# Two attention loops: one group of filler products per round, second-half value products issued in the next round

## What is computed

```
# first block, per block of 128 queries, branches c, s, w
p = softmax(where(mask, q @ k.T * scale, NEG));  o_b = p @ v
o = g[0] * o_c + g[1] * o_s + g[2] * o_w
mix = sigmoid(gate_a) * (o @ w_proj_a) + sigmoid(gate_b) * (ret_out @ w_proj_b)
# second block
p = softmax(q @ k.T * scale + F[q] - F[k]);  ya = p @ v           # fox, causal
sel = top_k(sum_h iw * relu(iq @ ik.T), 128);  yb = softmax(q @ k[sel].T * scale) @ v[sel]   # dsa
merged = sigmoid(ga) * (ya @ w_br_fox) + sigmoid(gb) * (yb @ w_br_dsa)
```

## Time and profile before

| | us |
|---|---|
| median of 3 runs (lowest, highest) | 2024.86 (2023.76, 2025.74) |
| the profiled execution | 2024.89 |
| its span in the trace | 2022.7 |
| TensorE busy | 1979.8 |
| VectorE, ScalarE, GpSimd busy | 930.9, 729.3, 794.3 |
| first attention, on TensorE | about 222.8 to 382.1 |
| second attention, on TensorE | about 1370.3 to 1534.7 |

### The profile page before, as it was taken

One profiled execution on the slowest core, in us unless ns is written; L12 is line 12 of the kernel. 1 busy time (PEld: TensorE's weight loads), 2 busy tenths in 40 slices (PEclk: granted clock), 3 DMA queues, 4 the chain that ended last, 5 costly groups with the idle time before them and its releaser, 6 DMA issues.

```text
span 2022.7 us, 25626 instructions
## 1 busy us (share of the span) xinstructions
PE 1979.8 (98%) x9324; PEld 1564.7 (77%) x9324; DVE 930.9 (46%) x1506; ACT 729.3 (36%) x1203; POOL 794.3 (39%) x329
## 2 busy tenths in 40 slices
PE   7999999999999999999999999999999999999998
PEld 6777666688888888888888887775757888888887
DVE  6763566432642563567761105586992341101111
ACT  5233455433431332332323224526453342221321
POOL 4365321243554345344543443231113434444442
PEclk9999999999999999999999999999999999999999
DMA  6345111243666477548533342231112424343341
GB/s 180 84 124 137 42 42 43 48 105 103 170 157 193 125 182 200 138 128 211 164 96 89 92 111 70 56 84 42 37 48 53 106 71 103 84 115 90 87 111 55
DMA packets 154565, 211.14 MB, mean 104 GB/s; under 512 B 15432, under 2 KB 129640, under 8 KB 154344
## 3 DMA queue, kind: packets, MB, share of 16 engines
q1 hardware_dynamic: 140232, 167.34, 33.1%
q10 hardware_dynamic: 14240, 42.54, 7.0%
HBM read 206.69 MB, written 2.10 MB: 103 GB/s over the span
## 4 chain that ended last, share of the span: by engine, by line
PE 49%; issue 31%; POOL 12%; DVE 7%; ACT 1%; DMA 0%; POOLq 0%; ACTq 0%; DVEq 0%
PE ps L628 15%; PE ps L630 15%; PE ps L629 15%; POOL wlo L594 12%; DVE top L2266 1%; DVE score L2268 1%; DVE ps L2157 1%; PE ps L1085 1%; PE ps L1108 0%; PE ps L719 0%; DVE PT L1987 0%; DVE Pb L1987 0%; PE ps L1311 0%; PE ps L1128 0%; DVE st L1902 0%
## 5 line engine op out<-in xcount | busy, mean ns | idle before, releaser
L594 POOL TENSOR_TENSOR wlo<-raw,whi 128x1024 fp32r<-128x1024 f32 (+1 forms) x317 | 784.0, 2490 | 1175.2 <-ACT whi L1377 1152.8
L628 PE MATMUL ps<-hhi,whi 128*128 128x512 f32 x1488 | 589.4, 396 | 6.6 <-DVE hlo L1896 2.7
L630 PE MATMUL ps<-hhi,wlo 128*128 128x512 f32 x1488 | 580.7, 390 | 0.0
L629 PE MATMUL ps<-hlo,whi 128*128 128x512 f32 x1488 | 580.2, 390 | 0.0
L1377 ACT ACTIVATE whi<-raw 128x1024 fp32r<-128x1024 f32 x309 | 316.9, 1055 | 378.9 <-PE ps L630 368.2
L628 PEld LDWEIGHTS ps<-hhi,whi 128*128 128x128 f32 x1488 | 280.0, 188 | 71.9 <-issue 9.9
L630 PEld LDWEIGHTS ps<-hhi,wlo 128*128 128x128 f32 x1488 | 279.7, 188 | 59.3
L629 PEld LDWEIGHTS ps<-hlo,whi 128*128 128x128 f32 x1488 | 280.1, 188 | 57.3 <-issue 1.4
L628 PE MATMUL ps<-hidhi,whi 128*128 (+1 forms) x608 | 236.6, 389 | 0.0
L630 PE MATMUL ps<-hidhi,wlo 128*128 (+1 forms) x608 | 236.5, 389 | 0.0
L629 PE MATMUL ps<-hidlo,whi 128*128 (+1 forms) x608 | 236.5, 389 | 0.0
(11 more groups left out here) (376 smaller groups left out, 2374.1 us busy)
## 6 DMA issues: line engine op xcount, KB each, us to landing
raw<-in_ffn_w SPq DMA_DIRECT2D x264, 256.0 KB, 3.8
raw<-in_w_in SPq DMA_DIRECT2D x154, 256.0 KB, 3.9
trig<-in_ada_w ACTq DMA_DIRECT2D x72, 512.0 KB, 4.7
raw<-in_w_up SPq DMA_DIRECT2D x64, 256.0 KB, 3.9
raw<-in_w_down SPq DMA_DIRECT2D x64, 256.0 KB, 4.0
raw<-in_w_out SPq DMA_DIRECT2D x32, 256.0 KB, 3.7
xrow<-in_x ACTq DMA_DIRECT2D x4, 512.0 KB, 6.8
raw<-in_cmp_k_w SPq DMA_DIRECT2D x8, 256.0 KB, 3.7
```

Source lines behind the costliest of these rows:

```text
L594: last = pool.tensor_tensor(lo, src, hi.bitcast(F32), ALU.subtract)
L628: pe.matmul(out_, lhi, rhi, start=first, stop=False)
L629: pe.matmul(out_, lhi, rlo, start=False, stop=False)
L630: return pe.matmul(out_, llo, rhi, start=False, stop=last)
```

## The change

Only TensorE's two loops over rounds are changed. In each round all four quarters (all of a round's quarters in the second attention, from round 2 on) go between the transposes and the values of the first half. The values of the second half of a round are put in a list, `late`, and issued in the next round, after its scores of pair 0 and ahead of its first transposes; what is left after the last round is issued at the end. In the second attention the order of index units is as before. No other engine's program is touched.

```diff
--- before.py
+++ after.py
@@ nsa_attention
                 n = len(UNITS1)
+                late = []
                 for r in range(n + 2):
                     nb = BLOCKS1[r - 2] if r >= 2 else 0
+                    half = (nb + 1) // 2
                     if r < n:
                         score_pair(r, 0)
                         if r == 0:
                             head_sum(3)
-                    half = (nb + 1) // 2
-                    for part, blocks in enumerate((range(half), range(half, nb))):
-                        if part == 1 and r < n:
-                            score_pair(r, 1)
-                            if r == 0:
-                                root_spread(3)
-                        for j in blocks:
-                            turn(r - 2, j)
-                        if r < n:
-                            branch_b(r, 2 * part, 2 * part + 2)
-                        for j in blocks:
-                            values(r - 2, j)
+                    for u, j in late:
+                        values(u, j)
+                    for j in range(half):
+                        turn(r - 2, j)
+                    if r < n:
+                        branch_b(r, 0, 4)
+                    for j in range(half):
+                        values(r - 2, j)
+                    if r < n:
+                        score_pair(r, 1)
+                        if r == 0:
+                            root_spread(3)
+                    for j in range(half, nb):
+                        turn(r - 2, j)
+                    late = [(r - 2, j) for j in range(half, nb)]
+                for u, j in late:
+                    values(u, j)
@@ fd_attention
                 n = len(UNITS2)
+                late = []
                 for r in range(n + 2):
                     nb = BLOCKS2[r - 2] if r >= 2 else 0
                     quarters = 4 * (FILL2[r + 1] - FILL2[r])
+                    half = (nb + 1) // 2
+                    first = quarters // 2 if r < 2 else quarters
                     if 2 * r < len(UNITS):
                         index_unit(2 * r)
                     if r < n:
                         score_pair(r, 0)
-                    half = (nb + 1) // 2
-                    for part, blocks in enumerate((range(half), range(half, nb))):
-                        if part == 1:
-                            if 2 * r + 1 < len(UNITS):
-                                index_unit(2 * r + 1)
-                            if r < n:
-                                score_pair(r, 1)
-                        for j in blocks:
-                            turn(r - 2, j)
-                        filler(r, quarters * part // 2, quarters * (part + 1) // 2)
-                        for j in blocks:
-                            values(r - 2, j)
+                    for u, j in late:
+                        values(u, j)
+                    for j in range(half):
+                        turn(r - 2, j)
+                    filler(r, 0, first)
+                    for j in range(half):
+                        values(r - 2, j)
+                    if 2 * r + 1 < len(UNITS):
+                        index_unit(2 * r + 1)
+                    if r < n:
+                        score_pair(r, 1)
+                    for j in range(half, nb):
+                        turn(r - 2, j)
+                    filler(r, first, quarters)
+                    late = [(r - 2, j) for j in range(half, nb)]
+                for u, j in late:
+                    values(u, j)
```

## The result

The changed kernel takes 2063.9 us (median of 4 runs, 2063.24 to 2066.05) against 2025.3 us before (2023.76 to 2026.12): 1.0197 times, 95% interval 1.0184 to 1.0209. It is 38.6 us slower. The profiled execution has a span of 2063.9 us and ran in 2066.05 us.

What follows compares the result with a forecast made beforehand. It took TensorE alone to bound the first attention, and VectorE and TensorE in turns the second. The first's 27.7 - 4.8 - 2.8 = +20.1 us and the second's +8.2 were added to 2024.9, giving 2053 us, range 2045 to 2062.

Steps and rivals of the forecast that it cites:

- wide range of 2037 to 2068: Whole kernel: the range in us said to take the forecast, rival 1 and the lower half of rival 2.
- rival 2: Both attentions: TensorE's clock falls in the stalls, 4 to 12 times at 1.7 us, 2060 to 2073, say 2065; chance 0.14.
- waiting scores: Each round's first score pair waits for the third exponential of the round before; 0.8 to 1.7 us each in the first attention.
- The stalls of the first attention: Rounds 1 to 22: TensorE's waits before first scores, 14.0 us without second-half transposes and 13.8 with them, 27.7 in sum.
- Both paths: What releases the awaited exponential: ScalarE's copies with second-half transposes (1.65 us stall, widest round), VectorE's reduction without (1.72).
- The merges: Two groups of quarter products become one, 2.93 us for 3.14; 4.8 us gained in 24 rounds of the first attention.
- Rounds 24 and 25: End of the first attention: no first scores and the same order of products as before, so no stall was counted.
- stall of 2.00 us without a fall: One TensorE stall in the earlier trace, up to 1484.60 us, with no clock fall after it; cited against rival 2.
- The second attention: VectorE's reductions come late from round 5, by 6.7 us in round 13; rounds 15 to 17 add about 1.5; +8.2 us.
- Rival 1: Second attention: VectorE hides the stalls and only round 5's 2 us stay; 2047 us; chance 0.17.
- Rival 3: First scores do not wait, so only the merges and the idle won back count, -7.6 us; 2017 us; chance 0.04.
- Rival 4: Whole kernel: the reorder does not reach the bound, stalls being about as large as gains; 2025 us; chance 0.02.

Runs made afterwards that it cites:

- first_only: The changed kernel with the earlier loop put back in the second attention, so only the first has the new order; 2051.85 us, ratio 1.0132.
- exp_first: The changed kernel with ScalarE's two exponentials ahead of its copies of the transposes in the second half, both attentions; 2055.3 us, ratio 1.0155.
- values_ahead: The changed kernel with the late second-half values issued ahead of the next first scores, in both attentions; 2049.74 us, ratio 1.0128.
- second_only: The changed kernel with the earlier loop put back in the first attention, so only the second has the new order; 2036.57 us, ratio 1.0059.
- dummies: The changed kernel with three useless products ahead of each first score pair of the first attention from round 1; 2059.11 us, ratio 1.017.
- dummies_both: The changed kernel with three useless products ahead of the first scores in both attentions; 2058.81 us, ratio 1.0171.
- three_one: The changed kernel with new order in the first attention only, its quarters split three and one around the second-half transposes; 2032.9 us, ratio 1.0049.

## Why the prediction was right, point by point

The forecast was 2053 us, in a range of its own of 2045 to 2062; measured were 2063.9, 1.9 us above that range. Only the wide range of 2037 to 2068, which takes in half of rival 2, holds it, and the number is nearer to rival 2's 2065. The direction and the mechanism of the waiting scores held. The size was 10 us too low, since four terms all erred to one side: the clock in the first attention (5.6 us, in no sum of the forecast), the end of that stage (1.4, put at nothing), the clock in the second, and the late waits there (together 4.2 by the profile).

- **The stalls of the first attention.** 27.7 us worked out, 27.8 measured, each kind within 0.03 us. The straight line between 31 and 512 keys held: 0.99, 1.23, 1.48 expected, 1.00, 1.24, 1.48 found. Both paths, copies and reduction, are shown apart by turning ScalarE's order round.
- **The merges.** A group of twelve takes 2.93 us (227.00 to 229.93), as worked out. The 24 groups take 74.1 us, 3.8 of them for the falls of the clock that run through three groups, and the 48 of before 75.7. So 5.3 us were gained where 4.8 were worked out.
- **"Rounds 24 and 25 ... their order of products is the same as before."** This step failed, by 1.4 us: the order of the two rounds is the same, but what stands ahead of them is not. Round 23's second group had stood between its exponentials and round 24. Now T1 follows S1 directly, and its copies stand behind two exponentials and the split of a slab on ScalarE. V1 waits 2.73 us, 1.29 before. ScalarE, then TensorE:

```profile
399.85 0.68 ACT L1568 ACTIVATE trig<-ps,nmax 128x512 f32<-128x512 f32 x1
...
400.51 1.05 ACT L1392 ACTIVATE whi<-raw 128x1024 fp32r<-128x1024 f32 x1
401.46 1.08 ACT L1576 ACTIVATE Pb<-ps 128x512 f32<-128x512 f32 x2
...
402.11 1.52 PE L1005 MATMUL ps<-Pb,vrow 128*64 128x256 f32 x8 [2.73 <-ACT Pb L1576]
```

- **The clock of the first attention** was left out of the forecast and priced as rival 2. It fell four times, for 5.6 us together, where the text said 4 to 12 times at 1.7 us over both attentions. The price was somewhat high: a fall takes 1.2 to 1.6 us, since part of the low stretch lies in a stall. The mistake was in the weight. The stall of 2.00 us without a fall was one case, and 22 waits give a fall many occasions; and of the three falls in the second attention of before the prediction read one (1421.8) and passed over the other two (1370.7 and 1503.8). Its sign for rival 2, a mean clock below 0.95, did not show either: four falls in this stage are a mean of 0.96. With the falls the stage closes: 27.8 - 4.8 - 2.8 + 1.4 + 5.6 = 27.2, and 27.1 were measured (26.7 with the 5.3 us measured for the merges).
- **The Trainium skill's rule** ("TensorE: Matmul & The Clock Gate", "A second HAM failure mode: psum-queue depth-cycling") spoke against the change, and this case's traces bear it out in part: the clock fell behind recurring idle of 0.8 to 1.7 us before the scores, and not there when useless products filled most of it. It is not regular: such falls are three in the change, two in first_only, one in exp_first and none in values_ahead, which idles for 23.4 us in the stage, the change for 28.0.
- **The second attention.** 8.2 us expected, 12.4 found (12.7 in second_only; 12.1 by its median). VectorE's first lag, in round 5, was given as 2.8 us and is 2.9; rounds 6 to 11 as 2.2, 2.9, 4.2, 5.5, 6.0, 6.0, and they are 2.3, 3.2, 4.7, 5.9 (second reduction of 8), 6.6, 6.8, all counted from round 4. The rest comes in rounds 12 to 15. In round 12 TensorE had waited 2.79 us for VectorE's selection, the clock fell, and the 24 products in one group ran through it; VectorE then waited 3.82 us, where 0.7 had been allowed for. TensorE, then VectorE:

```profile
1519.66 1.65 PE L1092 MATMUL ps<-dkT,dqT 64*128 64x384 f32 x4 [2.79 <-ACT trig L1631]
...
1529.98 0.92 PE L1092 MATMUL ps<-dkT,dqT 64*128 64x384 f32 x4
...
1531.03 0.57 DVE L2172 CUSTOM_DVE_ANT_0 ps<-ps,sel 128x384 f32<-128x384 f32 x1 [3.82 <-PE ps L1092]
```

  The lag is 10.6 us behind this, 11.7 in the second half of round 14, 13.7 in that of round 15 and 14.4 at the end of the stage, where 6.7 and some 1.5 more had been worked out. Less the 2.0 us by which rounds 0 to 3 are shorter than in before's trace (1.5 of them its own fall of the clock), these are the 12.4. S0 to S1 is 10.3 us in round 12 instead of the 7.4 of my terms. Before, that wait was 2.00 us and brought no fall, and only half the group stood between the two. A wait of VectorE of 2.6 us in this round is in second_only, dummies, dummies_both, values_ahead and exp_first too, each with S0 to S1 at 9.1 us and one fall of 3.4 us in that round, where the change has one of 6.8. So it is no accident of one run. That the clock makes the wait is read from the traces, not shown by an experiment: no kernel with the merged groups runs this round at the higher clock throughout.
- **Rival 1**, that VectorE hides the second attention, is out: second_only is 12 us above before, and 2 were its price. **Rival 3** is out: no stall was shorter than its chain. **Rival 4** as well. **Rival 2** is in part what happened, as said above.

## What to carry to other kernels

A group of filler between two steps of a chain is there for its place, not for its sum: before merging two groups, take from the trace the time from one step to the next (here 1.15 to 3.56 us) and look at what stands between them afterwards. Where an engine serves a ring of three buffers with two stages behind it, as here, each of the two gaps of a round needs its own cover (the one group cost the first attention 21.5 us in one place and some 16 in the other), and work that is put behind a wait covers nothing. Add to a sum of many short stalls the slow clock that they may bring (here 0 to 5.6 us on 21.5), and look for the large group that will run through it.

## What was not expected of the hardware

- In the first attention the lower clock came with stalls of 0.8 to 1.7 us that recur every 5 to 10 us, and behind one wait of 2.7 us at its end. The seven falls of the change and first_only cost 1.2 to 1.6 us each.
- The same order of work of TensorE gave four falls in this stage in one kernel and three in another, and filled idle none or one, so single executions differ by several us: those of three_one lie between 2030.66 and 2038.08.
- The clock also falls with no idle before it. In nine of the eleven traces it does so between the attentions; in the changed kernel at 880.6, behind 24 products of one column and eight of 128. TensorE was full from 876 to 880.5, and in the next window, full as well, the mean clock is 0.66:

```profile
876.74 2.74 PE L676 MATMUL ps<-cst,tmp 128*128 128x1 f32 x24
```

```profile
880.00:885.00 5.00, 5.00 (x20) 4.21 (x20) 3.17 (x4) 2.10 (x3) 3.79 (x2) 0.66 0.81 194
```
